# One transformer block and one hybrid layer on one core: the modulation sums on VectorE, the PEER output gain as columns, the last norms in one root

## The chip, the cores and the metric

The kernel runs on one core of a Trainium2 chip, as one program of five engine queues (TensorE, VectorE, ScalarE, GpSimd and SyncE, here PE, DVE, ACT, POOL and SP) that wait for each other by semaphores. The metric is the device time of one execution in microseconds. All data is 32-bit float. Lower is better.

## The reference, cut to what matters

256 tokens of width 1024 go through two layers. Cut to the lines that the change touches:

```python
mod = c_act @ w_mod + b_mod                        # c_act = silu(c), w_mod is 1024 x 6144
sh1, sc1, gt1, sh2, sc2, gt2 = split(mod, 6)       # six vectors of 1024
h = rmsnorm(x, ln_mix_g) * (1 + sc1) + sh1
proj = h @ w_in                                    # q, k, v of three attentions, gates, convolution
mixed = concat([rmsnorm(o_attn), rmsnorm(o_conv)])
x = x + gt1 * (mixed @ w_out)
h2 = rmsnorm(x, ln_ffn_g) * (1 + sc2) + sh2
# PEER: per token, 8 heads x 16 experts out of 16384, chosen by two top-16 lists
x = x + gt2 * sum_e(g_e * gelu(h2 . expert_u[e]) * expert_v[e])
y = rmsnorm(x, ln_final_g)                         # end of the first layer
hn = rmsnorm(y, pre_norm_w)                        # second layer: two branches on hn
...
return y + rmsnorm(out, post_norm_w)
```

`rmsnorm(x, g)` is `x * rsqrt(mean(x * x) + 1e-6) * g`.

## The kernel before, in words

All instructions of an engine run in the order in which the program lists them; a helper on line 88 records every one, so every row of the profile says L88 and the names of the tiles tell them apart. Tokens lie in two tiles of 128 (a = 0 and 1).

**Weights.** All weight matrices come as slabs of 8 x 128 rows by 512 columns (2.1 MB, two DMAs of 1 MB; one slab of `w_in` has 280 columns) through a ring of four slots `W`, in the order of a list `plan`. SP issues slab i + 4 once slab i has been used (`done_w`), and SP's own queue is in order.

**Head (0 to about 202 us).** The first four slabs of `w_mod` (sh1, sc1) are summed by PE and DVE together (`mod_halves`). Six more (sh2, sc2, gt1) are each summed on POOL by `mod_sum`: multiply the whole slab by c, then three adds that halve it. They stand in `plan` one behind each of the six slabs of `w_in`, whose projections PE computes between 41 and 152 us, with scores of the first attention units and the compression in between (`run_step`). DVE adds position terms to two banks of the block projection (`blk`), copies the four banks of `flip_bias`, and adds biases to scores. A PSUM bank is taken in turn from a ring of eight (`ps`), and PE waits for whoever read it last. Then `attn_mm`, `mod_cols_sum` (turns a 512-wide sum into four columns by four matrix products of one column each), the norms, the first query projection and the first selection (`route`), whose scratch `sw` lies in the row table of gt2, `R_G2`.

**Gather stage (202 to 915 us).** For each of 256 groups of 128 experts POOL issues a gather of 1.05 MB (128 rows of 2048 floats, u and v) into one of at most seven buffers `AR`; DVE takes the dot product with h2; ACT computes gelu, the weight, and a small diagonal; PE adds the weighted v rows in two banks of 512 columns (`combine`, two groups per step p, 128 steps; steps 0 to 63 are tile 0). A buffer goes back to the ring when PE has read it. Beside that run the rest of the attention of tile 1, and the route of both tiles. When the second route ends, gt2 is made as rows: the table `rows[3]` is loaded into `R_G2` and `mod_row` multiplies the slabs 10 and 11 of `w_mod` by c, spread over 128 rows (16 products of 512 columns on PE), and DVE adds the table. Only then `x2_steps(0)` starts: residual, first norm (dot, root, one fused multiply), second norm (dot, root, multiply); `norm_T` turns it, and `qk_project` computes queries and keys of tile 0 in steps 86, 92, 98 and 104, eight products of 512 columns at once each. The table of the post norm, `rows[1]`, is loaded in the loop once the eighth key score is done.

**Tail (915 to 1403 us).** The queries and keys of tile 0 are turned (`rope_turn`), `x2_steps(1)` runs on DVE, then the projections of tile 1 and the second layer.

Of the kernel before, what the change touches and what calls it, by code (L numbers as in the profile page):

```python
# [113 lines left out]
def build(nc, x, cst, oh, pc, cmpw, keysT, rel, rows, ab, w_mod, w_in, w_out, wq, puv,  # L114
          w_in2, wba, wbb, wo2, out, scr):
    ctx = ExitStack()
    with ctx:
# [45 lines left out]
        for (a, n), m in zip(((0, 512), (512, 512), (1024, 280), (1304, 512), (1816, 512), (2328, 512)), (6, 7, 8, 9, 4, 5)):  # L163
# [131 lines left out]
        def mod_sum(buf, free):  # L295

            i, w, t_w = next_w()
            gtt = nc.gpsimd.tensor_tensor
            t = G(gtt, w[:, :, :], w[:, :, :], cs.unsqueeze(2).to_broadcast([P, 8, 512]), MUL, after=[t_w, t_cs])
            t = G(gtt, w[:, 0:4, :], w[:, 0:4, :], w[:, 4:8, :], ADD, after=[t])  # L300
            t = G(gtt, w[:, 0:2, :], w[:, 0:2, :], w[:, 2:4, :], ADD, after=[t])
            t = G(gtt, buf, w[:, 0, :], w[:, 1, :], ADD, after=[t] + free)
            done_w(i, t)
            return t
# [16 lines left out]
        def mod_row(r, n):  # L321
# [9 lines left out]
            return b.free[0]  # L331

# [59 lines left out]

        def feat(w, cols, rhs, t_w, t_r, b, o, m=P):

            for k in range(8):
                t = PE(mm, b.t[0:m, o:o + S], cols(w, k), rhs[:, k, :], start=(k == 0), stop=(k == 7),
                       after=b.old + [t_w] + t_r)
            return t
# [4 lines left out]
        def token(w, c, n, rhs, a, t_w, t_r, b, o):  # L403
            for k in range(8):
                t = PE(mm, b.t[:, o:o + n], rhs[:, k, a * 128:a * 128 + 128], w[:, k, c:c + n],
                       start=(k == 0), stop=(k == 7), after=b.old + [t_w] + t_r)
# [4 lines left out]
        ms_buf = [RT[:, 512 * n:512 * n + 512] for n in range(3)] + [R_POST[:, 0:512], R_POST[:, 512:1024], R_LNF[:, 0:512]]  # L411

        def mod_next():
            n = len(t_ms)
            t_ms.append((ms_buf[n], mod_sum(ms_buf[n], [])))
# [12 lines left out]
        mod_next()  # L428

        i, w, t_w = next_w()  # L430
        t_blk = [[], []]
# [18 lines left out]
        mod_next()  # L450
# [10 lines left out]
        mod_next()  # L461
# [217 lines left out]
        for n, dst in enumerate((cbT, ccT, None)):  # L679
            i, w, t_w = next_w()  # L680
            for j2 in range(2):
# [11 lines left out]
                if j2 == 1:  # L693
                    done_w(i, t)
                    mod_next()
                run_step(2)
                if (n, j2) == (2, 0):
# [106 lines left out]
        def q_project(a, m, js=(0, 1)):  # L804
# [5 lines left out]
            for j in js:  # L810
                q = 2 * (m % 2) + j
                for k in range(8):
                    t = PE(mm, b.t[:, j * 128:j * 128 + 128], w[:, k, q * 128:q * 128 + 128], hT[:, k, c],
                           start=(k == 0), stop=(k == 7), after=b.old + [t_w] + t_hx[a])
# [224 lines left out]
        for n in range(4):  # L1039
            t_mc.append(mod_cols_sum(b2, 4 * n, *t_ms[n]))  # L1040
# [927 lines left out]
```

How the kernel before makes its waits and increments, by code:

```python
    def emit(self, eng):  # L79
        seen = {}
        for after, f, args, kw, tok, inc in self.items:
            for t in after:
                if seen.get(t.sem.name, 0) < t.value:
                    eng.wait_ge(t.sem, t.value)
                    seen[t.sem.name] = t.value
            if f is None:
                continue
            ins = f(*args, **kw)
            if inc == 16 or tok.used:
                ins.then_inc(tok.sem, inc)
```

## Time and profile before

| | us |
|---|---|
| median of 3 runs | 1398.9 |
| lowest and highest | 1396.18, 1405.27 |
| the profiled execution | 1404.89 |
| its span, first to last instruction | 1403.1 |
| PE busy in the span | 1154.9 (82%) |
| DVE busy | 743.8 (53%) |
| ACT busy | 485.0 (35%) |
| POOL busy | 363.9 (26%) |

The profiled execution lies 6.0 us above the median, so a sum of differences in its rows is set against 1404.89 and then carried to the median. The shares are averages over three stages with different limits; each stage has to be read by itself, first by the windows, then by what ends each wait.

### The profile page before, as it was taken

The numbers are of one execution on the slowest core, as the hardware profiler recorded it, in microseconds if no ns is written. First come the engines' busy times: TensorE is split into PE (matmuls) and PEld (weight loads), VectorE is DVE, ScalarE is ACT, GpSimd is POOL, SyncE is SP. The second block draws the span as 40 slices with busy tenths as digits, with TensorE's granted clock in tenths as the row PEclk, the third lists the DMA queues.
The fourth block names the chain that finished last, engine by engine and source line by source line (L and its number), as shares of the span: only waits on it lengthen the run. The fifth ranks groups of instructions, "written<-read, shape, count | busy, mean of one in ns | idle before, by whom it ended". The sixth has DMA issues, their size and how long they took to land.

```text
span 1403.1 us, 15272 instructions
## 1 busy us (share of the span) xinstructions
PE 1154.9 (82%) x5688; PEld 673.4 (48%) x5688; DVE 743.8 (53%) x1808; ACT 485.0 (35%) x1282; POOL 363.9 (26%) x285
## 2 busy tenths in 40 slices
PE   6999968878787678666677766779988998999997
PEld 2888653332342123111122211134867887899883
DVE  5132658888639994465444455430466567642111
ACT  1131124463424452344332233321577544113101
POOL 0888013333334543333343334300000000000000
PEclk9989967998898999899999998889999999999999
DMA  9965418999999999999999999914413131114130
GB/s 392 326 260 212 162 71 324 361 351 401 396 412 421 415 418 394 415 421 422 422 394 405 395 396 421 422 69 181 180 61 117 63 121 62 62 61 180 60 120 31
DMA packets 57094, 378.70 MB, mean 270 GB/s; under 512 B 7187, under 2 KB 10428, under 8 KB 11964
## 3 DMA queue, kind: packets, MB, share of 16 engines
q0 software_dynamic: 36864, 268.45, 47.2%
q1 hardware_dynamic: 19488, 107.23, 20.2%
q10 hardware_dynamic: 668, 2.04, 0.4%
q8 instruction: 45, 0.74, 0.2%
q14 instruction: 29, 0.24, 0.0%
HBM read 376.64 MB, written 1.06 MB: 269 GB/s over the span
## 4 chain that ended last, share of the span: by engine, by line
PE 51%; DMA 21%; DVE 17%; ACT 7%; issue 3%; POOL 1%; ACTq 0%; POOLq 0%; DVEq 0%
PE ps L88 51%; DMA AR<-in_puv,idx 20%; DVE AR L88 8%; DVE RT L88 3%; ACT L88 2%; ACT av L88 1%; DVE rowb L88 1%; DVE hT L88 1%; DVE acc L88 1%; POOL AR L88 1%; DMA X<-in_x 1%; ACT acc L88 1%; ACT rowb L88 1%; DVE junk L88 1%; ACT AR L88 1%
## 5 line engine op out<-in xcount | busy, mean ns | idle before, releaser
L88 PE MATMUL ps<-AR,acc 128*64 128x512 f32 x912 | 355.5, 704 | 172.0 <-ACT acc L88 171.0
L88 POOL DMA_INDIRECT AR<-in_puv,idx x256 | 271.3, 1060 | 491.7 <-PE ps L88 395.9
L88 PE MATMUL ps<-hT,W 128*128 128x256 f32 (+1 forms) x1472 | 318.0, 374 | 4.2 <-ACT rowb L88 3.0
L88 PEld LDWEIGHTS ps<-hT,W 128*128 128x128 f32 x1472 | 268.5, 198 | 54.7 <-issue 15.4
L88 PEld LDWEIGHTS ps<-AR,acc 128*64 128x64 f32 x912 | 85.9, 150 | 414.1 <-ACT acc L88 335.3
L88 DVE CUSTOM_DVE_ANT_0 AR<-AR,mixT 128x1024 f32<-128x1024 f32 x128 | 156.9, 1228 | 155.1 <-DMA AR<-in_puv,idx 154.9
L88 DVE CUSTOM_DVE_ANT_0 AR<-AR,tok 128x1024 f32<-128x1024 f32 x128 | 153.0, 1220 | 58.4 <-DMA AR<-in_puv,idx 58.3
L88 ACT ACTIVATE av<-av 128x1 f32<-128x1 f32 x256 | 51.3, 200 | 314.2 <-DVE av L88 314.0
L88 ACT ACT_TABLE_LOAD x104 | 133.4, 1283 | 12.8 <-DVE PT L88 11.0
L88 PE MATMUL ps<-W,hT 128*128 128x512 f32 (+3 forms) x288 | 98.0, 498 | 0.8 <-ACT hT L88 0.8
L88 ACT ACTIVATE acc<-fold,av 128x64 f32<-128x64 f32 x228 | 79.3, 348 | 7.4
L88 ACT ACTIVATE av<-av,gwp 128x1 f32<-128x1 f32 x256 | 75.4, 295 | 8.3
L88 PEld LDWEIGHTS ps<-W,hT 128*128 128x128 f32 x288 | 48.6, 194 | 49.1 <-issue 47.8
L88 ACT ACTIVATE PT<-ps 128x512 f32<-128x512 f32 (+1 forms) x44 | 21.6, 496 | 122.2 <-PE ps L88 121.6
L88 PE MATMUL ps<-AR,mixT 128*64 128x512 f32 x112 | 46.6, 747 | 20.9 <-ACT mixT L88 20.8
L88 ACT ACTIVATE AR<-ps 128x512 f32<-128x512 f32 (+5 forms) x51 | 22.9, 467 | 117.9 <-PE ps L88 117.8
L88 PE MATMUL ps<-AR,W 128*128 128x256 f32 x256 | 57.5, 381 | 0.0
L88 POOL TENSOR_TENSOR W<-W,st 128x4096 f32<-128x4096 f32 x6 | 42.1, 7016 | 47.1 <-DMA W<-in_w_mod 47.1
L88 PEld LDWEIGHTS ps<-AR,W 128*128 128x128 f32 x256 | 48.2, 190 | 6.6
L88 PE MATMUL ps<-AR 64*64 64x15 f32 (+4 forms) x416 | 49.7, 291 | 0.3
L88 PEld LDWEIGHTS ps<-AR 64*64 64x64 f32 (+2 forms) x416 | 39.9, 199 | 9.4 <-issue 2.7
L88 POOL TENSOR_TENSOR W<-W 128x2048 f32<-128x2048 f32 (+1 forms) x12 | 42.7, 3561 | 0.9
(231 smaller groups left out, 1092.3 us busy)
## 6 DMA issues: line engine op xcount, KB each, us to landing
W<-in_w_in SPq DMA_DIRECT2D x50, 1024.0 KB, 6.9
W<-in_w_mod SPq DMA_DIRECT2D x24, 1024.0 KB, 11.7
W<-in_w_out SPq DMA_DIRECT2D x4, 1024.0 KB, 5.9
W<-in_wq SPq DMA_DIRECT2D x4, 1024.0 KB, 8.1
AR<-in_puv,idx POOLq DMA_INDIRECT x256, 11.3
W<-in_wba SPq DMA_DIRECT2D x4, 1024.0 KB, 6.1
W<-in_wbb SPq DMA_DIRECT2D x4, 1024.0 KB, 7.0
W<-in_wo SPq DMA_DIRECT2D x4, 1024.0 KB, 6.0
```

Of the source, the lines that this page charges most:

```text
L88: ins = f(*args, **kw)
```

## The change

- The modulation sums move from POOL to DVE: `mod_sum_v` is a chain of eight instructions of 512 columns on one slab (one multiply, seven multiply-adds). There are now eight of them, with slabs 10 and 11 (gt2) too, and the order of slabs in `plan` is new. The places of the sums in DVE's order are chosen by where `mod_next` is called.
- gt2 is now columns: `mod_cols_sum` for two more slabs, one add of the bias, and, after the second route, `spread_g2` twice (four products of 128 columns with the identity, one copy to `R_G2`). `mod_row` and the load of `rows[3]` go.
- `feat`, `token` and `q_project` wait for the one block of `hT` that they read.
- `x2_steps` takes both norms from two sums of squares (of x and of x times ln_final_g) that ACT computes by halves; the factor for the second norm is one root of both sums, and the first norm's result is written later. It starts on the first half of a bank pair when that half is ready (`combine` returns both ends).
- The queries and keys of tile 0 are computed in 16 pieces, one per step p, each two products of 512 columns (`qk_piece`).
- In the tail a square root on one number stands ahead of `x2_steps(1)`, and the copies of the turned queries and keys stand behind the root of the norm. The load of `rows[1]` is written behind the loop.

```diff
-        for (a, n), m in zip(((0, 512), (512, 512), (1024, 280), ...), (6, 7, 8, 9, 4, 5)):
-            plan += [(w_in, a, n), (w_mod, m * 512, 512)]
+        mods = [(w_mod, m * 512, 512) for m in (6, 7, 8, 9, 4, 5, 10, 11)]
+        plan += [cuts[0], mods[0], mods[1], cuts[1], mods[2], cuts[2], mods[3], cuts[3], mods[4], mods[5],
+                 cuts[4], mods[6], cuts[5], mods[7]]
         plan += [(w_out, 0, 512), (w_out, 512, 512), (wq, 0, 512), (wq, 512, 512)]
-        for n in (10, 11):
-            plan.append((w_mod, n * 512, 512))
...
+        def mod_sum_v(buf):
+            i, w, t_w = next_w()
+            t = V(ts_, buf, w[:, 0, :], cs[:, 0:1], None, MUL, after=[t_w, t_cs])
+            for k in range(1, 8):
+                t = V(stt, buf, w[:, k, :], cs[:, k:k + 1], buf, MUL, ADD, after=[t])
+            return i, t
...
+        def spread_g2(n, after):
+            b = ps.take()
+            for j in range(4):
+                t = PE(mm, b.t[:, j * 128:j * 128 + 128], g2c[:, 4 * n + j:4 * n + j + 1].to_broadcast([P, P]), ident,
+                       start=True, stop=True, after=b.old + [t_g2c])
+            e = A(act, R_G2[:, n * 512:n * 512 + 512], b.t[:, :], ACT.Copy, after=[t] + after)
...
         done_w(i, t)
-        mod_next()
+        done_w(*mod_next())
+        done_w(*mod_next())
         i, w, t_w = next_w()
+        third = mod_next()
         t_blk = [[], []]
...
+        for n in range(2):
+            t_mg2 = mod_cols_sum(b2, 16 + 4 * n, *t_ms[6 + n])
...
             for n in range(2):
                 c = slice(n * 512, n * 512 + 512)
-                t = V(tt_, junk[:, c], E[a][n].t[:, :], R_G2[:, c], MUL, after=[t_acc] + t_g2 + ([t] if n else free))
+                t = V(tt_, junk[:, c], E[a][n].t[:, :], R_G2[:, c], MUL, after=[t_acc[n]] + t_g2 + free)
                 t = V(tt_, X[:, a, c], X[:, a, c], junk[:, c], ADD, after=[t])
+                t_sum.append(A(act, PT[:, 1, 0:512], X[:, a, c], ACT.Square, accum_out=sums[:, 0, n:n + 1], after=[t] + x2_sq[0]))
+                t = V(tt_, junk[:, c], X[:, a, c], R_LNF[:, c], MUL, after=[t, t_rows[0]])
+                t_sum.append(A(act, PT[:, 1, 512:1024], junk[:, c], ACT.Square, accum_out=sums[:, 1, n:n + 1], after=[t] + x2_sq[1]))
-            t = V(ttr, junk[:, :], X[:, a, :], X[:, a, :], 1.0 / D, EPS, MUL, ADD, r1, after=[t])
-            t = A(act, r1, r1, ACT.Sqrt, after=[t])
-            t = V(rec, r1, r1, after=[t])
-            t_x2[a] = V(stt, X[:, a, :], X[:, a, :], r1, R_LNF, MUL, MUL, after=[t, t_rows[0]])
-            t = V(ttr, junk[:, :], X[:, a, :], X[:, a, :], 1.0 / D, EPS, MUL, ADD, r2, after=[t_x2[a]])
...
+            t_tot = V(tt_, tot, sums[:, :, 0], sums[:, :, 1], ADD, after=t_sum)
+            t = V(ts_, e, tot[:, 0:1], EPS / D, EPS * EPS, MUL, ADD, after=[t_tot])
+            t = V(stt, q, tot[:, 1:2], 1.0 / D, e, MUL, ADD, after=[t])
+            t = A(act, q, q, ACT.Sqrt, after=[t])
+            t = V(rec, q, q, after=[t])
+            t_xb2[a] = V(ts_, tok2[:, a, :], junk[:, :], q, None, MUL, after=[t, t_lastdot[a]])
...
-                load_row(3, [t_idx[1, 7], t_gw[1, 7]])
-                for n in range(2):
-                    t_g2.append(mod_row(3, n))
+                spread_g2(0, [t_idx[1, 7], t_gw[1, 7]])
...
-            if p in (86, 92, 98, 104):
-                m = (p - 86) // 6
-                qk_project("qk"[m % 2], 0, m // 2, [t_tp, t_gw[1, 7]])
+            if t_hb and len(qk_done) < 16:
+                m, k0 = divmod(len(qk_done), 4)
+                qk_done.append(qk_piece("qk"[m % 2], m // 2, 2 * k0, [t_tp, t_gw[1, 7]]))
...
-        rope_turn("q", 0)
-        rope_turn("k", 0)
-        for _ in x2_steps(1, t_pelast, t_rot["k", 0]):
-            pass
+        load_row(1, [t_keyfree[7]])
+        turned = [rope_turn_mm(kind, 0) for kind in "qk"]
+        A(act, st[:, 46:47], eps, ACT.Sqrt, after=[t_in])
+        last = x2_steps(1, e, t_rot["k", 0])
+        while t_xb2[1] is None:
+            advance(last, 1)
+        for kind, u in zip("qk", turned):
+            rope_turn_copy(kind, 0, u)
```

Three places of the order of instructions show what moves. The first is DVE in the head, after `norm_T` has written `hT`: the sums into `RT` and `rowb`, the position adds (`AR<-ps,AR`), the copies of `flip_bias` (`acc<-ps`); s_w0 to s_w3 are the semaphores of the four weight slots. Of the kernel after the change:

```order
L88 TENSOR_SCALAR RT<-W,st 128x512 [waits s_w2]
L88 SCALAR_TENSOR_TENSOR RT<-W,st,RT 128x512 [waits s_dve] x7
L88 TENSOR_SCALAR RT<-W,st 128x512 [waits s_w0]
L88 SCALAR_TENSOR_TENSOR RT<-W,st,RT 128x512 [waits s_dve] x7
L88 TENSOR_TENSOR AR<-ps,AR 128x240 [waits s_cw,s_pe]
...
L88 COPY kcT<-ps 128x15 [waits s_pe]
L88 TENSOR_SCALAR rowb<-W,st 128x512 [waits s_w3]
L88 SCALAR_TENSOR_TENSOR rowb<-W,st,rowb 128x512 [waits s_dve] x7
L88 COPY vc<-ps 15x64 [waits s_pe]
```

Before, the position adds followed `hT` directly and the copy of `vc` followed that of `kcT`; now a sum that waits for its slab stands ahead of each. The second place is SP in the gather stage. Before:

```order
L88 DMA W<-in_w_in2 128x2048 [waits s_pe]
L88 DMA W<-in_w_in2 128x2048
L88 DMA rowb<-in_rows 128x1024 [waits s_pe]
L88 DMA rowb<-in_rows 128x1024 [waits s_dve]
L88 DMA W<-in_w_in2 128x2048 [waits s_pe]
```

After the change, with the last slab that is loaded in the loop ahead of the row table, and the first slab of the tail behind it:

```order
L88 DMA W<-in_w_in2 128x2048 [waits s_pe]
L88 DMA W<-in_w_in2 128x2048
L88 DMA rowb<-in_rows 128x1024 [waits s_pe]
L88 DMA W<-in_w_in2 128x2048 [waits s_pe]
```

One row table, `rows[3]`, has gone; the other, `rows[1]`, still waits for PE's eighth key score and nothing on SP stands between the last slab of the loop and it. The third place is PE in the head, between the output projection (`W,mixT`) and the sums of squares of the convolution (`AR,K`), one piece of the difference:

```order
 L88 MATMUL ps<-W,mixT 128x512 x16
 L88 MATMUL ps<-K,RT 128x1 x12
-L88 MATMUL ps<-K,rowb 128x1 x4
+L88 MATMUL ps<-K,rowb 128x1 x12
 L88 MATMUL ps<-AR,K 128x128 x4
```

Eight products of one column more stand ahead of the norm's sums (the trace counts each 32-bit product as two instructions).

## Rows read from the trace of the kernel before

**Rows 1.** Chain that ended last: start us, length us, what

```profile
40.71 112.17 PE ps L88 x740
154.82 22.69 PE ps L88 x84
916.95 1.95 PE ps L88 x6
```

**Rows 2.** Windows, gather stage: us, engines' busy us (instructions), PEclk, DMA share, GB/s

```profile
555.00:560.00 5.00, 5.00 (x22) 1.73 (x18) 3.17 (x6) 3.18 (x11) 3.62 (x3) 0.88 0.86 321
650.00:655.00 5.00, 3.00 (x8) 0.66 (x8) 2.47 (x4) 1.72 (x7) 2.94 (x4) 1.00 1.01 421
655.00:660.00 5.00, 3.97 (x8) 1.04 (x8) 2.47 (x4) 1.72 (x7) 1.80 (x2) 0.66 1.01 419
715.00:725.00 10.00, 7.47 (x26) 2.35 (x26) 5.06 (x8) 5.23 (x21) 5.80 (x6) 1.00 0.88 327
750.00:755.00 5.00, 3.20 (x12) 0.75 (x9) 2.47 (x4) 1.73 (x7) 3.76 (x4) 1.00 0.89 310
780.00:790.00 10.00, 7.48 (x28) 2.30 (x25) 3.80 (x6) 4.16 (x16) 6.08 (x6) 0.92 0.87 327
810.00:820.00 10.00, 7.30 (x26) 2.27 (x26) 5.03 (x9) 5.38 (x20) 5.43 (x6) 1.00 0.88 338
```

**Rows 3.** Timeline where gt2 is made: start us, us, engine, operation, idle before

```profile
535.42 14.00 PE L88 MATMUL ps<-W,st 128*128 128x512 f32 x32
542.59 7.67 SPq L88 DMA_DIRECT2D W<-in_w_in  x4
555.75 0.94 POOL L88 DMA_INDIRECT AR<-in_puv,idx  x1 [18.59 <-PE ps L88]
```

**Rows 4.** Timeline, one query projection of tile 0

```profile
706.85 7.13 PE L88 MATMUL ps<-W,hT 128*128 128x512 f32 x16
```

**Rows 5.** DVE groups by shape: count, busy us, mean ns, idle before

```profile
L88 DVE SCALAR_TENSOR_TENSOR hT<-W,st,hT 128x256 f32<-128x256 f32 x28 | 13.6, 485 | 1.0
L88 DVE SCALAR_TENSOR_TENSOR X<-X,st,rowb 128x1024 f32<-128x1024 f32 x2 | 2.6, 1282 | 0.0
L88 DVE TENSOR_SCALAR AR<-RT,PV 128x256 f32<-128x256 f32 x24 | 8.4, 349 | 21.0 <-ACT RT L88 21.0
```

**Rows 6.** Timelines of the head, DVE, PE, POOL and SP

```profile
66.76 1.35 DVE L88 TENSOR_TENSOR AR<-ps,AR 128x240 f32<-128x240 f32 x4 [27.07 <-DMA AR<-in_cmpw]
73.71 3.62 PE L88 MATMUL ps<-hT,W 128*128 128x256 f32 x16
74.40 7.02 POOL L88 TENSOR_TENSOR W<-W,st 128x4096 f32<-128x4096 f32 x1 [3.92 <-DMA W<-in_w_mod]
113.25 0.80 SPq L88 DMA_DIRECT2D W<-in_w_in  x2
124.07 7.07 PE L88 MATMUL ps<-hT,W 128*128 128x256 f32 x32
```

**Rows 7.** DMA issues: engine, count, KB each, median us to landing

```profile
W<-in_w_in SPq DMA_DIRECT2D x50, 1024.0 KB, 6.9
```

**Rows 8.** Timeline, one-column products to the root of the norm

```profile
171.24 2.73 PE L88 MATMUL ps<-K,RT 128*128 128x1 f32 x24
173.83 1.74 PE L88 MATMUL ps<-K,rowb 128*128 128x1 f32 x8
177.53 0.37 ACT L88 ACTIVATE AR<-ps,K 128x128 f32<-128x128 f32 x1 [21.18 <-PE ps L88]
```

**Rows 9.** Windows, the same place

```profile
174.00:177.50 3.50, 3.49 (x16) 3.19 (x15) 0.46 (x4) 0.00 (x0) 0.00 (x0) 0.50 0.00 0
```

**Rows 10.** Timeline of the last norm

```profile
918.92 0.69 DVE L88 TENSOR_TENSOR junk<-ps,rowb 128x512 f32<-128x512 f32 x1 [2.96 <-PE ps L88]
926.54 0.75 DVE L88 TENSOR_SCALAR tok<-X,st 128x1024 f32<-128x1024 f32 x1
```

**Rows 11.** ACT group that holds the squares of 512 columns

```profile
L88 ACT ACTIVATE tok<-ps 128x512 f32<-128x512 f32 x12 | 6.8, 592 | 66.1 <-PE ps L88 66.1
```

More of the change, by code:

```diff
@@ L391, in build, with of_k @@
         t_h, t_xn = norm_T((0, 1), tok_at, t_xb, sc1, sh1, [t_m1])
+        def of_k(t_r, k):
+            return t_r[k:k + 1] if len(t_r) == 8 else t_r
         def feat(w, cols, rhs, t_w, t_r, b, o, m=P):
@@ L449, in build @@
         done_w(i, t)
-        mod_next()
+        done_w(*third)
         t_B = flip_bias()
@@ L680, in build @@
             i, w, t_w = next_w()
+            if n == 2:
+                done_w(*mod_next())
             for j2 in range(2):
@@ L694, in build @@
                     done_w(i, t)
-                    mod_next()
+                if (n, j2) == (0, 1):
+                    done_w(*sixth)
+                elif j2 == 0 and n < 2:
+                    done_w(*mod_next())
                 run_step(2)
+                if (n, j2) == (0, 0):
+                    sixth = mod_next()
                 if (n, j2) == (2, 0):
@@ L813, in q_project @@
                     t = PE(mm, b.t[:, j * 128:j * 128 + 128], w[:, k, q * 128:q * 128 + 128], hT[:, k, c],
-                           start=(k == 0), stop=(k == 7), after=b.old + [t_w] + t_hx[a])
+                           start=(k == 0), stop=(k == 7), after=b.old + [t_w, t_hx[a][k]])
             if js[-1] == 0:
@@ L1043, in build @@
         q_norm1(0)
-        sh2, sc2, t_m2 = mod_affine(b2, t_mc[3], 24, V_LNF, 16)
+        sh2, sc2, t_m2 = mod_affine(b2, t_mg2, 24, V_LNF, 16)
+        g2c = modc[:, 32:40]
+        t_g2c = V(tt_, g2c, b2.t[:, 16:24], PV[:, V_BMOD + 40:V_BMOD + 48], ADD, after=[t_mg2, t_pc])
+        b2.free = b2.free + [t_g2c]
         q_norm2(0, [])
@@ L1167, in qk_project, with qk_piece @@
             t_rot.setdefault((kind, a), []).append(e)
+        qk_bank = {}
+        def qk_piece(kind, n, k0, free):
+            if (kind, n) not in wqk:
+                wqk[kind, n] = next_w()
+            i, w, t_w_ = wqk[kind, n]
+            if k0 == 0:
+                qk_bank[kind, n] = ps.take()
+            b = qk_bank[kind, n]
+            for k in (k0, k0 + 1):
+                t = PE(mm, b.t[:, :], hT[:, k, 0:P], w[:, k, :], start=(k == 0), stop=(k == 7),
+                       after=b.old + [t_w_, t_hb[0][k]])
+            if k0 == 6:
+                e = A(act, rot[kind, 0][:, n * 512:n * 512 + 512], b.t[:, :], ACT.Copy, after=[t] + free)
+                b.free = [e]
+                t_rot.setdefault((kind, 0), []).append(e)
         def rope(kind, a, free):
@@ L1209, in combine @@
                         ring.append([n, [e]])
-            return e
-        ahead = []
+                ends.append(e)
+            return ends
+        ahead, qk_done = [], []
         h1 = half1()
@@ L1279, in build, with rope_turn_mm @@
         t_rope, t_turn = {}, {}
-        def rope_turn(kind, a):
-            dst = qaT if kind == "q" else kaT
-            toks = []
+        def rope_turn_mm(kind, a):
+            turned = []
             for h4 in range(2):
@@ L1289, in rope_turn, with rope_turn_copy @@
                            after=b.old + t_rot[kind, a])
+                turned.append((h4, b, t))
+            t_turn[kind, a] = t
+            return turned
+        def rope_turn_copy(kind, a, turned):
+            dst = qaT if kind == "q" else kaT
+            toks = []
+            for h4, b, t in turned:
                 e = A(act, dst[:, 4 * h4:4 * h4 + 4, a * 128:a * 128 + 128], b.t[:, :].rearrange("p (h t) -> p h t", h=4),
@@ L1304, in build @@
         t_hball = t_hb[0] + t_hb[1]
+        advance(last, 9)
         for n in range(2):
```

66 lines of the change are left out of this document (35 added, 31 removed).

## The prediction

> **What bounds the kernel now.** I read the chain of waits first, to find the three stages, then windows of each stage, then the timeline where a window falls short. In the head the chain is PE's: 112 us of products in one piece from 40.71, then 22.7 us more up to the norm of the first residual [rows 1]. PE has no idle time to give there, so anything that makes it wait moves the first gather. In the gather stage a normal window shows the limit: DMA share 1.01 at 421 GB/s, while PE is busy 3.0 of 5 us and DVE 2.5 [rows 2]. A gather of 1.05 MB at 421 GB/s takes 2.49 us, a pair (one step p) 4.98. The stage is paid for in bytes and in windows in which the DMA runs below 421. Behind the last product at 918.9 [rows 1] DVE and ACT alone work until PE turns the normed tile; then PE bounds again.
>
> **The change part by part.** The sum is made against the profiled execution (1404.89 us, span 1403.1) and then carried to the median, 6.0 lower.
>
> *1. The sums leave POOL; what they cost DVE.* One sum is one multiply and seven multiply-adds on 512 columns. The rows have 485 ns at 256 and 1282 at 1024 columns [rows 5]; on the line between them 512 columns take 0.75 us, and the multiply, from 349 ns at 256 [rows 5] and 0.75 us at 1024 [rows 10], 0.48. With some 0.03 us between dependent instructions a sum is 6.0 us. Eight are 48 us, and DVE has room for that between 40 and 152. POOL's own work was on no path. So the price is not the work but the place: DVE runs in order, and a sum waits for its slab.
>
> First place, the third sum, ahead of the position adds. Its slab landed at 74.4 before, when POOL waited for it [rows 6], behind a slab of 1.15 MB (280 columns) that is now behind it: 1.15 MB at 421 is 2.7 us, so it lands at 71.7 if nothing else changes, and at the earliest at 69.4, its own 2.1 MB sooner. I take 70.5, about the middle. Then 6.0 for the sum and two adds of 0.34 [rows 6] free the bank of the block projection at 77.2. PE's next projection, eight banks later in the ring and so in this very bank, began at 73.71 [rows 6]: PE is held **3.5 us** longer. Ends: nothing if DVE gets the slab earlier than any of this, and 7.4 with a landing at 74.4. The wait by blocks of `hT` lets PE start about a microsecond sooner at 40.7; that goes into this hold and counts nothing.
>
> Second place, the seventh sum, between the copies of `kcT` and `vc`. Its slab is issued when the first convolution projection is done, where a slab was issued at 113.25 [rows 6]; it lands 6.9 us after the second half's issue [rows 7], at about 120.6, and the sum and one copy end at 126.7. The projection that takes the bank of that copy began at 124.07 [rows 6]: **2.6 us**, between nothing and 6.3 if a sum takes 9.7 us, the price at 1024 columns. The other sums end in time: the fourth before the copies it shares DVE with are missed, the fifth and sixth under 15 us of compression on PE, the eighth ahead of a projection that ends later.
>
> Third place, one-column products. Before the norm's sums stand 16 more PE instructions of this kind. The row has 24 of them in 2.73 us, and the next 8 in 1.74, because the granted clock fell to 0.50, the level of 1.2 GHz [rows 8, 9]: at this level 16 take **3.5 us**, at the full one 1.8. They are on the path: ACT's root waits for PE there [rows 8], and the second root, of the residual, is behind it in ACT's queue. I take 3.5, as the first 24 already end at the fall. The Trainium skill (TensorE: Matmul & The Clock Gate, The HAM clock gate) says that the throttled state is the default. By that rule the level to which the row has fallen stays for the products that come next, which gives 3.5 too; with all of them at the level of the first 24 the sum would be 1.7 lower.
>
> Head: 3.5 + 2.6 + 3.5 = **+9.6**.
>
> *2. What leaves the gather stage.* Two slabs of 2.1 MB and one row table of 0.52 MB, 4.72 MB in all, go into the head or go entirely. At 421 GB/s that is **-11.2 us**. For 18.59 us up to 555.75 POOL issues no gather, released by PE at last, because 14.0 us of 32 instructions stand in PE's queue ahead of the combine, and SP loads the two next slabs from 542.59 on, once those are read [rows 3]. So in this hole the DMA moves the very bytes that go, and the hole and the bytes must not be counted twice. Only the part in which the DMA was short is added: the window at 555 has 321 instead of 421 GB/s [rows 2], 0.50 MB, **-1.2**. `spread_g2` puts eight narrow products and two copies there, hidden under 2 us of PE's slack per pair. The Trainium skill (DMA: Bandwidth & Descriptors, Where 436 GB/s comes from) puts the limit of HBM for one core at about 358 GB/s; by it the bytes would be worth 13.2. The windows here show 421 for hundreds of microseconds, so I keep 11.2.
>
> *3. The row table of the post norm.* It is written behind the loop, but on SP nothing stands between the last slab of the loop and it, and it waits for the eighth key score as before. It will be issued at the same time, inside the gather stage: **0**. If it did leave, 0.52 MB would be worth 1.2 us.
>
> *4. Queries and keys in pieces.* Before, a burst of 16 instructions held PE for 7.13 us [rows 4], four times. After each the DMA ran short: 94 GB/s for 10 us, 111 for 5, 94 for 10 and 83 for 10 below 421 [rows 2], 3.27 MB together, 7.8 us. A piece is four of these 16 instructions, 1.8 us, and a pair then needs 3.0 + 1.8 = 4.8 us of PE in 4.98. The piece stands between a combine and the next, whose last group lands 2.5 us after its first, so no buffer comes back later. **-7.8**, between 0 (the shortfall only spreads) and that.
>
> The new squares, roots and the earlier start of `x2_steps(0)` lie under the gathers; ACT is busy 1.7 of 5 us there [rows 2].
>
> *5. The last norm.* From the end of the combine to the end of DVE's last multiply it was 918.89 to 927.29 [rows 1, 10]. Now the first half starts after two of the last six instructions, at 917.6; six DVE instructions of 0.69 us [rows 10] and gaps end at 921.9; the squares, 0.6 us each on ACT [rows 11] plus a read of the accumulator, end at 922.8; three small sums, root and reciprocal (about 0.2 each, ACT's table already loaded) and the multiply of 0.75 give 924.7: **-2.6**. Ends: 0 if ACT has the copies or a table load ahead of the root, -3.3 if the squares hide wholly.
>
> Sum: 9.6 - 11.2 - 1.2 - 7.8 - 2.6 = **-13.2**, 1391.7 for the profiled execution, **1386** from the median.
>
> **The rivals.**
>
> *B, DVE's queue is dearer (0.13).* The slab lands at 74.4, and a sum takes 9.7: the first hold is 11.1, the second 6.3, the columns 3.5, the head +20.9; the total is -1.9, **1397**. For it: DVE also waits for DMA in the head. Against it: the slab has less ahead of it than before.
>
> *C, the bursts don't pay (0.13).* The pieces cost the DMA as much as the bursts: -5.4, **1393 to 1394**. For it: 4.8 of 4.98 us is tight. Against it: PE had 2 us to spare in each pair.
>
> *D, the sums hold nobody (0.13).* Slabs land early enough, only the columns cost, at the full clock, and the early start at 40.7 counts: head +0.6, total -22.2, **1377**. For it: the landing is the least certain number here. Against it: the first hold needs the slab more than 2.4 us earlier than 69.4's bound allows.
>
> *E, slower: the pieces make PE the bound of the gather loop (0.05).* Place: the 16 pairs with a piece. In some windows the clock is granted at 0.66 on average and the same 8 instructions take 3.97 us [rows 2]; with a piece at half clock (3.6) a pair takes 7.5 us of 4.98, 2.5 more for each of 16 pairs, 40. A burst of 7.13 us lost about 1.9, so 5.2 are absorbed by what is queued: +35, in place of none, total +22, **1421**. It is slower than before from about seven such pairs on. Against it: with PE full the window at 715 has clock 1.00 [rows 2].
>
> *F, the post norm's table does leave the stage (0.03):* -14.4, **1384 to 1385**. Against it: the order on SP.
>
> **How the numbers follow.** My forecast (A) has 0.53 and a range of its own of 1380 to 1392, from the ends of the first two holds. A change of 1% is 14.0 us, about what a measurement of this kernel can tell; its bounds are 1384.9 and 1412.9. Faster by over 1%: all of D, 0.13, half of F, 0.02, and a little less than half of A, 0.24, and 0.02 of C: 0.41. Slower by over 1%: most of E, 0.04, and 0.01 of B. The rest, 0.54, is within 1%. The range has to hold A, C and most of B and D: 1376 to 1399 leaves out E, a third of B and some of D, under 2 in 10.
>
> **What would show it right or wrong.** In the head: PE's wait for DVE before the projection that began at 73.71, and again before the one at 124.07, and the first gather near 211.7 instead of 202.1; without such waits D holds. One-column products: 48 instructions in about 7.9 us. In the gather stage: no gap in POOL's issues near 540, no window under 400 GB/s where the pieces run, and the time from first gather to last landing shorter by 20; shorter by 12 is C, longer is E. A row table still landing near 515 refutes F. At the end: 7 us between the last combine and the end of the multiply of `tok`, measured from the first half. The forecast is wrong if the first gather comes more than 5 us off, or if PE's clock falls while the pieces run.

## The result, and the profile after

The changed kernel takes **1395.42 us** (median of 20 runs, 1384.93 to 1400.21) against 1401.38 for the kernel before in the same comparison (20 runs, 1395.85 to 1408.70): ratio 0.9948, 95% interval [0.9932, 0.9964]. It is half a per cent faster, inside the range and within the 1% that a measurement was said to tell apart, but the forecast of 13.2 us less came out as about 6. In a second comparison it was 1391.42 against 1400.3, 0.9937 [0.9919, 0.9955].

The profiled execution took 1396.34 us (span 1394.5), 8.6 less in span than the one of before. Three rows cut each span into four parts: the issue of the first gather on POOL, the transfer of the last gather in the chain of waits (start, length), and PE's first product of the normed tile. Timeline and chain of the kernel before (start us, us, engine or transfer, operation, idle before and what ended it):

```profile
202.06 1.12 POOL L88 DMA_INDIRECT AR<-in_puv,idx  x1 [60.76 <-DVE gw L88]
903.42 11.28 DMA AR<-in_puv,idx
927.44 1.94 PE L88 MATMUL ps<-K,tok 128*128 128x128 f32 x8 [6.66 <-DVE tok L88]
```

And of the kernel after:

```profile
215.99 1.08 POOL L88 DMA_INDIRECT AR<-in_puv,idx  x1 [215.14 <-DVE gw L88]
901.84 11.27 DMA AR<-in_puv,idx
924.09 1.06 PE L88 MATMUL ps<-K,tok 128*128 128x128 f32 x8 [3.25 <-DVE tok L88]
```

Read as differences, this is the table that the rest of the text uses. The experiments are in it too, each read from its own three rows:

| profiled execution | first gather issued | gather stage | last landing to normed tile | from there to the end |
|---|---|---|---|---|
| before | 202.1 | 712.6 | 12.7 | 475.7 |
| after | 216.0 | 697.1 | 11.0 | 470.4 |
| after, second profile | 215.6 | 692.2 | 10.4 | 472.1 |
| seventh sum behind | 209.0 | 694.6 | 10.4 | 475.3 |
| third sum behind | 214.2 | 689.2 | 10.4 | 474.2 |
| products in the wait | 214.0 | 693.3 | 10.9 | 470.5 |
| head, all three | 214.1 | 691.9 | 10.4 | 474.7 |
| bursts back | 216.7 | 698.2 | 10.4 | 475.3 |
| slower routing | 215.3 | 693.9 | 11.3 | 472.6 |
| head as before | 201.0 | 704.4 | 10.7 | 475.1 |
| copies ahead again | 215.1 | 693.9 | 11.9 | 472.1 |
| order of slabs | 203.0 | 685.5 | 10.4 | 474.6 |
| same, routing as changed | 200.9 | 692.2 | 10.4 | 474.5 |
| same, output slab first | 199.2 | 688.8 | 10.4 | 474.4 |

So the head **lost 13.9 us** (forecast 9.6), the gather stage **gained 15.5**, in a second profile 20.4 (forecast 20.2), and the norm behind it 1.8 to 2.4 (forecast 2.6). The last column spreads by 5 us (470.4 to 475.3) between kernels whose code is the same there: PE's 2842 instructions in it are busy 447.6 us after the change, at a mean granted clock of 0.97, and 453.8 in "seventh sum behind", at 0.96. So the 5.3 us by which the first profile of the change ends sooner than before are not shown to be a gain of the change.

Where the head lost it, PE's timeline after the change shows (start us, us, products, idle before). Rows of before that answer to those at 77.70 and 131.67 are [rows 6]:

```profile
66.21 3.60 PE L88 MATMUL ps<-mixT,K 128*128 128x512 f32 x8
77.70 6.24 PE L88 MATMUL ps<-hT,W 128*128 128x256 f32 x16 [7.89 <-DVE AR L88]
83.77 4.30 PE L88 MATMUL ps<-W,hT 128*128 128x152 f32 x32
118.86 7.17 PE L88 MATMUL ps<-hT,W 128*128 128x256 f32 x32
131.67 10.01 PE L88 MATMUL ps<-hT,W 128*128 128x256 f32 x32 [2.38 <-DVE vc L88]
142.39 7.07 PE L88 MATMUL ps<-hT,W 128*128 128x256 f32 x32
184.36 4.48 PE L88 MATMUL ps<-K,rowb 128*128 128x1 f32 x24
197.96 5.89 PE L88 MATMUL ps<-hT,W 128*128 128x128 f32 x32
```

Three rows of before: those at 70.27 and 184.70 answer to the first and the last of these, the one at 103.10 has no wait ahead of it and is long all the same:

```profile
70.27 3.60 PE L88 MATMUL ps<-mixT,K 128*128 128x512 f32 x8
103.10 10.12 PE L88 MATMUL ps<-hT,W 128*128 128x256 f32 x32
184.70 5.21 PE L88 MATMUL ps<-hT,W 128*128 128x128 f32 x32
```

Both forecast waits for DVE are there, and each row behind a wait is long by itself: 6.24 us for 16 instructions that took 3.62 before [rows 6], 10.01 for 32 that took 7.07 [rows 6] and take 7.07 again at 142.39. The first wait is 7.89 us long though the products start only 4.0 later than before, because PE came to it 4.1 sooner (66.21 against 70.27). A long row alone does not prove a wait, as the one at 103.10 shows (granted clock 0.70 there), so the experiments below take the waits away. The windows of these two places (length, busy us of PE, its weight loads, DVE, ACT, POOL, then granted clock, DMA share, GB/s) show why:

```profile
70.00:77.70 7.70, 0.00 (x0) 0.00 (x1) 6.43 (x11) 0.00 (x0) 0.00 (x0) 0.67 1.03 422
77.70:84.00 6.30, 6.30 (x18) 5.18 (x19) 6.16 (x11) 0.03 (x1) 0.00 (x0) 0.59 1.01 423
131.60:141.60 10.00, 9.93 (x33) 8.18 (x34) 7.52 (x21) 2.38 (x10) 0.00 (x0) 0.71 0.56 210
```

The granted clock fell while PE waited and was still near its lower level (0.50 is 1.2 GHz) for most of the products behind the wait. DVE's side is as priced: the third sum begins at 71.02 (forecast 70.5), and the sum lasts 5.9 us (forecast 6.0).

```profile
71.02 0.49 DVE L88 TENSOR_SCALAR RT<-W,st 128x512 f32<-128x512 f32 x1 [19.66 <-DMA W<-in_w_mod]
71.54 5.48 DVE L88 SCALAR_TENSOR_TENSOR RT<-W,st,RT 128x512 f32<-128x512 f32 x7
76.93 1.34 DVE L88 TENSOR_TENSOR AR<-ps,AR 128x240 f32<-128x240 f32 x4
```

In the gather stage the POOL gap of 18.59 us [rows 3] is gone (the longest from 500 to 565 is 5.60), and the windows in which the bursts ran [rows 2] are full, 419 to 422 GB/s at 710, 720, 750, 780 and 810; so is every 10 us from 640 to 720, where the pieces stand, at a granted clock of 1.00. One shortfall stands at 530 to 555, with DVE full in its first part and POOL waiting for PE:

```profile
530.00:535.00 5.00, 4.64 (x24) 2.65 (x22) 4.89 (x19) 0.29 (x1) 1.60 (x2) 0.66 0.97 382
535.00:540.00 5.00, 3.43 (x8) 1.07 (x8) 4.80 (x13) 4.71 (x10) 0.28 (x1) 0.68 0.93 364
540.00:545.00 5.00, 4.56 (x21) 1.56 (x19) 4.90 (x10) 3.26 (x13) 4.07 (x3) 0.98 0.48 162
```

The row table of the post norm was issued at 514.26, inside the gather stage, as forecast; the rival that it leaves the stage fell. In the tail ACT does the four squares beside DVE's six instructions of 512 columns, and the copies of queries and keys stand behind the root (timeline after, ACT):

```profile
921.32 0.63 ACT L88 ACTIVATE PT<-junk 128x512 f32<-128x512 f32 x1
922.75 0.20 ACT L88 ACTIVATE st<-st 128x1 f32<-128x1 f32 x1 [0.71 <-DVE st L88]
922.86 2.04 ACT L88 ACTIVATE AR<-ps 128x512 f32<-128x512 f32 x4
```

### The profile page after: what moved, and what is told of

It reads as the page before. It is cut to its first block, busy times and chain, and to the rows that moved or that the text cites. A ratio compares the mean times of both kernels' runs of the same rounds, so it can differ in the third digit from the quotient of the medians.

```text
span 1394.5 us, 15315 instructions
## 1 busy us (share of the span) xinstructions
PE 1149.9 (82%) x5688; PEld 667.8 (48%) x5688; DVE 775.7 (56%) x1875; ACT 491.4 (35%) x1301; POOL 277.2 (20%) x261
## 4 chain that ended last, share of the span: by engine, by line
PE 48%; DMA 24%; DVE 16%; ACT 7%; issue 4%; POOL 1%; ACTq 0%; SPq 0%; POOLq 0%; DVEq 0%
PE ps L88 48%; DMA AR<-in_puv,idx 21%; DVE AR L88 8%; DVE RT L88 3%; DMA W<-in_w_mod 2%; ACT L88 2%; ACT av L88 2%; DVE rowb L88 1%; ACT acc L88 1%; DVE acc L88 1%; POOL AR L88 1%; DMA X<-in_x 1%; ACT rowb L88 1%; DVE junk L88 1%; ACT mixT L88 1%
## 5 line engine op out<-in xcount | busy, mean ns | idle before, releaser
L88 PE MATMUL ps<-AR,acc 128*64 128x512 f32 x912 | 361.9, 704 | 162.7 <-ACT acc L88 159.5
L88 POOL DMA_INDIRECT AR<-in_puv,idx x256 | 276.9, 1082 | 625.0 <-PE ps L88 376.1
L88 PEld LDWEIGHTS ps<-hT,W 128*128 128x128 f32 x1472 | 270.4, 200 | 63.8 <-issue 13.9
L88 DVE SCALAR_TENSOR_TENSOR AR<-RT,PV,AR 128x256 f32<-128x256 f32 x72 | 34.9, 484 | 2.6
L88 PEld LDWEIGHTS ps<-AR,mixT 128*64 128x64 f32 x112 | 10.6, 153 | 45.1 <-ACT mixT L88 33.8
```

The lines of the kernel that those rows point to most:

```text
L88: ins = f(*args, **kw)
```

## The experiments

Each was timed in five rounds beside the kernel before; ratios are to that kernel in the same comparison, with 95% intervals. The change has 0.9948 and 0.9937. The first four expectations count from 217.37, and that of the head as before from 711.2; both are read from the second gather, whose issue is 1.4 us behind the first. Differences are not touched by that.

**The second hold.** The seventh sum goes behind the compression steps, that is, behind the copy of `vc`.

```
-                elif j2 == 0 and n < 2:
+                elif (n, j2) == (0, 0):
                     done_w(*mod_next())
                 run_step(2)
+                if (n, j2) == (1, 0):
+                    done_w(*mod_next())
```

> The seventh sum goes behind the compression steps that run after the first projection of the second third, so the copy of vc no longer waits for it. Theory 1: PE's idle 2.38 us before 131.67 goes, and the 32 instructions there take 7.07 in place of 10.01; first gather 5.3 sooner than 217.37, 1390 us. Theory 2: the wait moves to the eighth sum or to the next slab, first gather less than 2 us sooner, 1393.5 to 1395.5.

Measured 1385.55 us, 0.9892 [0.9865, 0.9919], below the change, with an interval that ends where the second one of the change begins. PE's row has no wait and its old length:

```profile
129.21 7.07 PE L88 MATMUL ps<-hT,W 128*128 128x256 f32 x32
137.00 7.07 PE L88 MATMUL ps<-hT,W 128*128 128x256 f32 x32
```

The projection at 142.39 begins at 137.00, 5.4 sooner (forecast 5.3), and the first gather comes 7.0 sooner. A wait of 2.4 us had cost more than twice its length. The other 1.7 us come from the 24 one-column products, which take 2.82 here in place of 4.48:

```profile
178.97 2.82 PE L88 MATMUL ps<-K,rowb 128*128 128x1 f32 x24
```

**The first hold.** The third sum goes behind the position adds and the copies of `flip_bias`, and the slab of 280 columns (`cuts[2]`) is loaded ahead of the sum's.

```
-        plan += [cuts[0], mods[0], mods[1], cuts[1], mods[2], cuts[2], mods[3], cuts[3], ...
+        plan += [cuts[0], mods[0], mods[1], cuts[1], cuts[2], mods[2], mods[3], cuts[3], ...
...
-        third = mod_next()
...
         t_B = flip_bias()
         i, w, t_w = next_w()
+        third = mod_next()
```

> The third sum goes behind the position adds and the copies of flip_bias, and the slab of 280 columns is loaded ahead of its slab. Theory 1 (two holds of PE by DVE, and after each a clock that has fallen, make the head late): PE's idle 7.89 us before the projection at 77.70 goes and the same 16 instructions take 3.6 again in place of 6.24, so the first gather comes 6.6 us sooner than at 217.37, up to 10 sooner if the smaller slab also lands earlier; 1385 to 1389 us against 1395.4 of the change. Theory 2 (the head is late because its weight slabs follow each other at the limit of the DMA and DVE has 48 us of sums in its one queue, so a hold that is taken away comes back at the next slab): first gather less than 2 us sooner, 1393.5 to 1395.5.

Measured 1390.38 us, 0.9942 [0.9915, 0.9969], not to be told from the change, as theory 2 had it. The 16 instructions take 3.62 again, as theory 1 had it, but PE's timeline has another hold in the place of the first:

```profile
71.36 3.62 PE L88 MATMUL ps<-hT,W 128*128 128x256 f32 x16
74.82 4.30 PE L88 MATMUL ps<-W,hT 128*128 128x152 f32 x32
83.43 9.43 PE L88 MATMUL ps<-hT,W 128*128 128x256 f32 x32 [4.31 <-DMA W<-in_w_in]
```

Here PE waits for the next slab of `w_in`, which two slabs of `w_mod` (`mods[2]` and `mods[3]`) precede; from 66 to 79 the DMA moves 421 to 424 GB/s, so the slab could not land sooner in this order. And again the row behind the wait is long, 9.43 in place of 7.07. So the first hold had two causes, one behind the other: DVE's order, and the order of the slabs. Taking away the first alone gives 1.8 us at the first gather.

**The clock by itself.** The first hold stays, but PE has 9 products in its queue for that time, which nobody reads:

```
+        for _ in range(9):
+            PE(mm, ps.banks[7].t[:, :], K[:, K_FLIP:K_FLIP + P], mixT[:, 6:8, :].rearrange("p h j -> p (h j)"),
+               start=True, stop=True, after=[t_vs, t_sk, t_in])
         i, w, t_w = next_w()
```

> The change with the first hold left as it is, but with 9 products of 128x512 that nobody reads (18 instructions, some 8 us) in PE's queue in the 7.89 us in which it waits. They leave the result as it is. If the clock that falls in the wait makes the next products dear: the 16 instructions behind the wait take 3.6 us in place of 6.24, the first gather comes about 2.5 us sooner (214.9), 1393 us. If those products are slow for another reason (their weights, the bank, DVE's sum beside them): 6.2 us as before, first gather at 217 to 218, 1395 to 1396.

Measured 1391.77 us, 0.9940 [0.9920, 0.9961]; as a time not to be told from the change. Timeline and windows decide:

```profile
66.55 11.32 PE L88 MATMUL ps<-mixT,K 128*128 128x512 f32 x26
78.47 3.72 PE L88 MATMUL ps<-hT,W 128*128 128x256 f32 x16 [0.60 <-DVE AR L88]
```

```profile
70.00:78.40 8.40, 7.87 (x19) 3.21 (x17) 6.37 (x11) 0.00 (x0) 0.00 (x0) 1.00 1.02 419
78.40:82.00 3.60, 3.53 (x16) 3.15 (x17) 3.56 (x9) 0.00 (x0) 0.00 (x0) 1.00 1.01 378
```

The products behind the same hold, with the same sum running on DVE, take 3.72 us in place of 6.24, at a granted clock of 1.00; the first gather comes 2.0 sooner. What made them long at this hold was the clock after an idle PE, not DVE, the bank or the weights. For the second hold there is no such run; its window above (0.71) says the same.

**The columns, with both holds.** Both edits above, and the 16 one-column products moved behind the query projections, into a bank of their own:

```
+        b3 = ps.take()
+        for n in range(2):
+            t_mg2 = mod_cols_sum(b3, 4 * n, *t_ms[6 + n])
+        g2c = modc[:, 32:40]
+        t_g2c = V(tt_, g2c, b3.t[:, 0:8], PV[:, V_BMOD + 40:V_BMOD + 48], ADD, after=[t_mg2, t_pc])
         while (0, 0) not in t_idx or (0, 0) not in t_gw:
```

> Both sums behind, and the 16 one-column products of slabs 10 and 11 moved behind the query projections, into a bank of their own. Theory 1: the terms add, 6.6 + 5.3 + 2.7 = 14.6 us, first gather at 202.8 or a little sooner, 1381 us (1377 to 1383). Theory 2: the weights and DVE's queue hold PE somewhere else, first gather after 210, 1388 us or more.

Measured 1389.38 us, 0.9919 [0.9892, 0.9945]; the first gather at 214.1, 1.9 sooner in place of the forecast 14.6, a miss by 12.7 us. Up to the first query projection PE is 10.2 us ahead of the change (187.77 against 197.96), with a wait of 4.62 us for a slab still in it, as with the third sum alone. Behind it the gain is lost to a new wait that the edit makes: DVE's `t_g2c` now stands ahead of the routing's steps and waits for the late products (8.77 us in the row below), and PE then waits 9.25 us for that routing.

```profile
201.30 1.84 PE L88 MATMUL ps<-K,rowb 128*128 128x1 f32 x16
203.18 0.17 DVE L88 TENSOR_TENSOR modc<-ps,PV 128x8 f32<-128x8 f32 x1 [8.77 <-PE ps L88]
212.40 0.61 PE L88 MATMUL ps<-RT,K 128*64 128x8 f32 x8 [9.25 <-DVE RT L88]
```

**The pieces.** The four bursts are put back.

```
-            if t_hb and len(qk_done) < 16:
-                m, k0 = divmod(len(qk_done), 4)
-                qk_done.append(qk_piece("qk"[m % 2], m // 2, 2 * k0, [t_tp, t_gw[1, 7]]))
+            if p in (86, 92, 98, 104):
+                m = (p - 86) // 6
+                qk_project("qk"[m % 2], 0, m // 2, [t_tp, t_gw[1, 7]])
```

> The change with the four bursts of 16 instructions put back at pairs 86, 92, 98 and 104 in place of the pieces. If the pieces gave the 7.8 us of the sum: windows of some 330 GB/s come back at four places, the time from the first gather's issue to the last landing is 7.8 longer than that of the change, 1403 us. Rival C (the bursts cost nothing, the gain of the gather stage came from the bytes alone): less than 2 us more, 1395 to 1397.

Measured 1399.60 us, 0.9993 [0.9971, 1.0014]: 0.0045 to 0.0056 above the change, 6 to 8 us, where 7.8 were forecast. The windows of before are back, of which the first and the last:

```profile
710.00:720.00 10.00, 8.52 (x27) 3.40 (x27) 4.97 (x8) 4.59 (x18) 1.34 (x2) 1.00 0.88 357
810.00:820.00 10.00, 7.51 (x26) 2.35 (x26) 4.61 (x7) 5.84 (x22) 4.72 (x5) 1.00 0.91 347
```

The five windows at 710, 720, 750, 780 and 810 are together 338 GB/s times 10 us short of 421, 8.0 us. Rivals C and E fall. The stage of this profile is only 1.1 us longer than that of the first profile of the change, but 6.0 longer than that of the second, which comes next.

**The shortfall at 530 to 555.** The change was profiled once more, unaltered.

> The changed kernel itself, profiled once more. If the shortfall of 4.6 us at 530 to 555 belongs to the change: the same windows fall under 400 GB/s again, and the time from the first gather's issue to the last landing is near 697 us again. If it is the scatter of single executions (the clock's phase against DVE's tightest pairs): 690 to 694 us, as in the experiments whose loop is the same. The head, whose order is fixed, should repeat to within 1 us: first issue at 215 to 217. 1394 to 1396 us.

Measured 1391.42 us, below the 1394 to 1396 expected. The stage took 692.2 us, and the windows there are

```profile
530.00:540.00 10.00, 5.93 (x22) 1.65 (x19) 9.69 (x30) 6.50 (x17) 5.56 (x5) 1.00 1.02 424
540.00:550.00 10.00, 7.47 (x40) 3.37 (x40) 7.29 (x16) 3.46 (x13) 6.34 (x6) 1.00 1.00 404
```

with one of 356 at 490 instead, there too at a granted clock under 1 (0.74). The first gather repeats within 0.4 us. So the loss of the head belongs to the change; the depth at 540 is the scatter of one execution, in a stretch where DVE is busy 4.9 of 5 us. That a slow clock on PE sets off such a dip is argued from these windows and not shown.

Its remedy, fewer routing steps per pair while tile 1 is routed:

```
-            advance(routes[0], 6 if p < 17 else 8)
+            advance(routes[0], 6 if p < 17 else 8 if p < 44 else 5)
```

> The routing of tile 1 advances by 5 steps in a pair instead of 8 from pair 44 on, so that it ends some 7 pairs later. Theory (the windows under 400 GB/s at 530 to 555, about 4.6 us, come from DVE: two dot products and 8 routing steps need more than the 4.98 us that a pair has on the DMA): the shortfall goes, 1391 us. Rival (it comes from PE's half clock there and the loads of ACT's table in the last routing steps, which stay): no change, 1395 us.

Measured 1391.89 us, 0.9928 [0.9902, 0.9955]. The windows from 530 to 560 have 418 to 422 GB/s, but the interval overlaps both of the change, and the stage (693.9) lies between its two profiles. The dips go, as the theory had it; as a time it is inconclusive.

**Head as before.** POOL sums, the old order of slabs and the two slabs in the gather stage come back; pieces, post norm and tail stay. One piece of the edit:

```
-                spread_g2(0, [t_idx[1, 7], t_gw[1, 7]])
+                load_row(3, [t_idx[1, 7], t_gw[1, 7]])
+                for n in range(2):
+                    t_g2.append(mod_row(3, n))
```

> The sums go back to POOL, the slabs and their order, the two slabs in the gather stage and the row table rows[3] are as before the change; the pieces, the new post norm and the tail stay as changed. Theory 1 (the head lost 13.9 us, the slabs and the row table gave back 11 to 12): first gather at 202 to 204, gather stage 7.8 shorter than the 711.2 before, tail 6.9 shorter, 1387 us, which is 8 below the whole change. Rival (the pieces pay only where the two slabs are out of the gather stage): 1394 us, about the whole change.

Measured 1390.06 us, 0.9925 [0.9898, 0.9951]: no slower than the whole change, perhaps a little faster, and between the two forecasts. The first gather comes 15.0 sooner than after the change and the stage is 7.3 to 12.2 longer; against the kernel before it is 8.2 shorter, which is the pieces (forecast 7.8). The part of the change that moves the sums to VectorE and the slabs to the head is thus worth nothing as it stands: it pays out what it takes in.

**The tail.** The copies of queries and keys go ahead again, and no root is evaluated early. The first piece of the edit:

```
-        turned = [rope_turn_mm(kind, 0) for kind in "qk"]
-        A(act, st[:, 46:47], eps, ACT.Sqrt, after=[t_in])
+        for kind in "qk":
+            rope_turn(kind, 0)
```

> The change without two edits of the tail: ACT copies the turned queries and keys ahead of the squares again, and no root is evaluated early, so its table is loaded where the first root stands. Theory (both stand in ACT's queue ahead of the norm: 2.06 us of copies and 1.28 of the table load): from the last landing to the first product of the normed tile 2.0 to 3.3 us more than the 10.4 to 11.0 of the runs so far, 1397.5 to 1398.5 us. Rival (DVE's six instructions of 0.69 set the end, ACT has the time): less than 0.5 more, 1395.5.

Measured 1395.35 us, 0.9966 [0.9949, 0.9983], about 4 above the change in the same comparison (1391.42), though the intervals overlap a little. ACT's rows show both costs, the copies ahead of the first square and the table load ahead of the root; DVE's first multiply here is at 912.27, so the squares begin 3.4 us behind it, against 1.4 after the change (917.10, 918.54):

```profile
913.71 2.06 ACT L88 ACTIVATE AR<-ps 128x512 f32<-128x512 f32 x4 [2.61 <-PE ps L88]
915.64 0.65 ACT L88 ACTIVATE PT<-X 128x512 f32<-128x512 f32 x1
918.22 1.28 ACT L88 ACT_TABLE_LOAD   x1
919.52 0.20 ACT L88 ACTIVATE st<-st 128x1 f32<-128x1 f32 x1
920.85 1.94 PE L88 MATMUL ps<-K,tok 128*128 128x128 f32 x8 [5.87 <-DVE tok L88]
```

From DVE's first multiply to PE's product it is 8.6 us here and 7.0 after the change: 1.6, and from the last landing 0.9 to 1.5, both below the forecast of 2.0 to 3.3, because the squares catch up with DVE. The other 2 us or so between the two medians are not in these rows.

**A version that beats both.** The slabs in the order of before with the two new ones at the end; the third and the seventh sum in DVE's queue behind the copies that free PE's banks; the one-column products behind those of the second norm, and the slower routing. The second sum stands ahead of the position adds, where the third stood after the change, but its slab lands at 49.60 and it holds nobody. Some of the added lines:

```
+        for u in range(6):
+            plan += [cuts[u], mods[u]]
+        plan += [mods[7], mods[6]]
...
         t_B = flip_bias()
...
+        third = mod_next(9)
...
+                if (n, j2) == (1, 0):
+                    seventh = mod_next(17)
...
         norm_root(("c", 1), nrm[:, 1, :], cbT[:, :, P:2 * P], t_oc[1])
+        b3 = ps.take()
+        for n in range(2):
+            t_mg2 = mod_cols_sum(b3, 4 * n, *t_ms[6 + n])
```

> A version that should beat both: the slabs in the order of the kernel before with the two new ones behind them, the second, third, seventh and eighth sum in DVE's queue behind the copies that PE's banks wait for, the 16 one-column products behind the products of the second norm where PE waits 1.63 us, and the slower routing from pair 44. Theory 1 (holds, and the clock after them): no wait of PE for DVE or for a slab before the output projection, first gather at 203 to 205, stage as in the change or 3 shorter, 1378 to 1382 us. Theory 2 (48 us of sums in DVE's one queue and 4.2 MB more in the head hold PE somewhere in any order): first gather at 208 or later, 1386 or more.

Measured **1375.75 us**, 0.9826 [0.9796, 0.9856]: 1.1 to 1.2% below the change and 1.0% below the version with the old head, faster than the 1378 to 1382 forecast. PE waits no more for DVE at either place; two waits for slabs are left, of which the one at 79.16 had been forecast to go:

```profile
69.70 3.62 PE L88 MATMUL ps<-hT,W 128*128 128x256 f32 x16
79.16 7.14 PE L88 MATMUL ps<-hT,W 128*128 128x256 f32 x32 [1.71 <-DMA W<-in_w_in]
128.17 7.07 PE L88 MATMUL ps<-hT,W 128*128 128x256 f32 x32
156.92 14.00 PE L88 MATMUL ps<-W,mixT 128*128 128x512 f32 x32 [2.74 <-DMA W<-in_w_out]
202.99 1.08 POOL L88 DMA_INDIRECT AR<-in_puv,idx  x1 [202.15 <-DVE gw L88]
```

Behind these two waits, 1.71 and 2.74 us long, the products keep their speed, 7.14 and 14.00 us where they take 7.07 and 13.90 without a wait: the granted clock was 1.00 in both waits and in the rows behind them. So not every wait brings slow products. The first gather is 13.0 sooner than in the change, with the same eight sums on DVE and the same bytes in the head. Two variants:

> The faster version without the slower routing, so 8 steps in a pair again. If the slower routing was worth what the windows of the change lacked: 2 to 4.6 us more than the 1375.75 of that version, with windows under 400 GB/s where the routing of tile 1 ends. If it was worth nothing: within 1.5 us of it.

Measured 1379.68 us, 0.9862 [0.9836, 0.9889]. This has the routing of the change and is still 0.7 to 0.9% below it, with intervals apart: the new orders, of the slabs and of the instructions in the head, beat the change by themselves. Against the version with the slower routing the intervals overlap, and the traces do not give the 4 us to the routing: from 440 to 600 both are about 1.9 us short of 421 GB/s (windows of 10 us below 421 added up), while 6.5 of the 6.7 us between their stages lie in the first 230 us of the stage, ahead of pair 44, where their code is the same.

> The faster version with the two slabs of w_out in the other order, so that the half that the output projection reads first takes the slot that comes free 30 us earlier. There PE waited 2.74 us for that slab. Theory (a weight's landing bounds the head at that place): the wait goes, first gather 2.7 sooner than 202.99, 1373 us. Rival (the next term, DVE's norm and ACT's roots, takes the wait's place): less than 1 us sooner, 1375.

Measured 1376.30 us, 0.9827 [0.9807, 0.9846]. The wait for `w_out` goes and the first gather is issued at 199.15, 3.8 sooner, but the time is the same: the rival's number, by another route, since the last gather lands only 0.6 us sooner (887.9 against 888.5). The first 230 us of the stage took 3.3 of it (21.9 us short of 421 GB/s in place of 18.6); whether that is scatter stays open.

## Why the prediction was wrong, step by step

**The head, forecast +9.6, measured +13.9: the step that failed.** The two holds were at the places named and of the size named: PE's start moved by 4.0 at the first (forecast 3.5), and the delay grew from 5.1 ahead of the second to 7.6 at its start, 2.5 (forecast 2.6). The step said that PE is held 3.5 and 2.6 us longer and let the products behind run at their old length. They did not: 2.6 us more behind the first, 2.9 behind the second, by the clock. That is 5.5 us that no term held; some 1.5 of the first came back before the second. The columns cost 2.7 (4.48 for 24 against 1.74 for 8 [rows 8]; forecast 3.5), and the first query projection behind them 0.7 (5.89 against 5.21, granted clock 0.64 and 0.73), which no term held either. The sum is 4.0 + 2.6 - 1.5 + 2.5 + 2.9 + 2.7 + 0.7 = 13.9. The early start, which the prediction put at a microsecond and into the hold, was 4.1 by 66.21; it made the first wait 7.89 us long. The prediction had even weighed the rule that bears on it, the Trainium skill (TensorE: Matmul & The Clock Gate, The HAM clock gate), which says that the throttled state is the default and activity lifts it, but for the columns alone and not for the products behind its own waits. The window of 0.59 and the products in the wait agree with that rule.

**The gather stage, forecast -20.2, measured -15.5 and -20.4.** The two slabs and the row table (-11.2 and -1.2) are seen in the version with the old head, whose stage is 7.3 to 12.2 longer than that of the change; the pieces (-7.8) in the bursts put back, 8.0 in windows. Eight profiles have the gather loop of the change (the two of it, the four runs on the head, "copies ahead again" and "same, routing as changed"): 689.2 to 697.1, 693.0 in the mean, which is 19.6 below the one profile of before. So the stage came as forecast, and the 15.5 is the far end of the scatter. Dips at the end of the routing are in every profile: from 440 to 600, by the windows of 10 us below 421 GB/s, the first profile of the change is 5.7 us short, the second 2.8, the kernel before 3.8 and the version with the old head 4.2. The moved slabs did not bring them. The largest loss of the stage is one that the change does not touch: its first 230 us run at 372 to 387 GB/s in all fourteen profiles, 19 to 27 us short of 421, and 5.5 of the 7.9 us between the longest and the shortest of the eight are there.

**The tail, forecast -2.6, measured -1.8 and -2.4 up to the normed tile.** Right; 1.6 of it is the copies and the table load.

**The basis.** 1386 was the sum laid on a median of three runs, 1398.9; with 20 runs the median before is 1401.38. Of the 9.4 us between 1386 and 1395.42 this is 2.5 and the head 4.3. The 2.6 that are left cannot be named: the profiled execution of before lay 3.5 above its median, stages of single profiles scatter by as much (the last column of the table), and the sum was made against one of them. In the second comparison the change is 8.9 below the kernel before, and what is missing to 13.2 is about the head's 4.3.

**The rivals.** B (holds of 11.1 and 6.3) was too dear at both places, though its 1397 came near by chance. So did the 1393 to 1394 of C, which fell with the bursts. D fell with the two waits, E with the windows (clock 1.00 and 419 to 422 GB/s where the pieces run), F with the issue at 514.26.

## What to carry to other kernels

A wait that an edit puts in front of the bounding engine can cost more than its length: here holds that delayed PE by 4.0 and 2.5 us cost another 2.6 and 2.9 in the products behind them, while waits of 1.71 and 2.74 in the last version cost no more than themselves. Read the row behind each wait, not the wait alone. When work moves to an engine with room, the question is not its busy time (48 us on DVE were free) but whose copy stands behind it, and which slab its own slab is loaded ahead of; the same sums in another order, with the one-column products at a place where PE waited, gave 13 us back at the first gather. And a stage read from one profile is one draw: eight profiles of the same loop spread by 8 us, more than most of the terms here.

## What the runs showed of the hardware

- PE's granted clock was 0.67 over 7.7 us in which PE did nothing and 0.59 over the 6.3 us behind them; filled with products that nobody read, the same stretch ran at 1.00, and 16 instructions took 3.72 in place of 6.24 us. Behind a wait of 2.38 us 32 instructions took 10.01 in place of 7.07, behind one of 4.31 they took 9.43; behind one of 2.74 the granted clock stayed at 1.00. No run here shows what parts the two cases.
- With POOL's sums gone, a DVE instruction of 128x4 elements in the head took 0.16 us; before, the same one took 3.99, 1.15 and 4.20 beside POOL's sums and 0.17 once they were over; with the sums back on POOL ("head as before") 5.77, 1.15, 1.15 and 0.17:

```profile
92.83 3.99 DVE L88 TENSOR_TENSOR sm<-sm,AR 128x4 f32<-128x4 f32 x1
```

- Gathers, with next to nothing else on the DMA, kept 420 to 424 GB/s in every 20 us from 560 to 900 after the change, so the figure of about 358 for one core that the Trainium skill gives (DMA: Bandwidth & Descriptors, Where 436 GB/s comes from) did not bind here.
- The last 470 to 475 us, the same code in the kernels made from the change, spread by 5 us between executions, and with them PE's busy time there, 447.6 to 453.8 us.
